# A two-block transformer kernel on one NeuronCore: the first feed-forward block moves from plain to Strassen products

## What is computed

```python
def swiglu(h, w_gate, w_up, w_down):
    return (jax.nn.silu(h @ w_gate) * (h @ w_up)) @ w_down

c_act = jax.nn.silu(c)
for l in range(DEPTH):                 # DEPTH = 2
    shift1, scale1, gate1, shift2, scale2, gate2 = jnp.split(c_act @ ada_w[l] + ada_b[l], 6, axis=-1)
    ...
    h = modulate(rms_norm(x, norm2_g[l]), shift2, scale2)
    x = x + gate2[:, None, :] * swiglu(h, ffn_w_gate[l], ffn_w_up[l], ffn_w_down[l])
```

## Time and profile before

| | |
|---|---|
| median of 3 runs | 1122.95 us (1122.59 to 1123.61) |
| the profiled execution | 1123.41 us |
| its span, first to last instruction | 1121.6 us |
| TensorE busy | 1059.0 us (94%) |
| VectorE busy | 577.9 us (52%) |
| ScalarE busy | 295.6 us (26%) |
| GpSimd busy | 64.0 us (6%) |
| mean granted TensorE clock | 0.987 |
| moved by DMA | 195.78 MB |

### The profile page before, as it was taken

The page is one execution under the profiler, slowest core; times in us unless marked ns, Lnnn a source line. Parts: engine busy times, 40 slices in busy tenths (PEclk is TensorE's granted clock), DMA queues, the critical chain, the costliest instruction groups (busy, mean ns, idle before and its releaser), DMA issues.

```text
span 1121.6 us, 21217 instructions
## 1 busy us (share of the span) xinstructions
PE 1059.0 (94%) x9229; PEld 910.9 (81%) x9229; DVE 577.9 (52%) x1112; ACT 295.6 (26%) x709; POOL 64.0 (6%) x84
## 2 busy tenths in 40 slices
PE   6878999999999999889999999999997899999997
PEld 4647888888888867678999999988886688887786
DVE  8986455344421727727766575335823551602632
ACT  6512410000000645623010000133322341202641
POOL 3010010110100100000000000000003000000000
PEclk9899999999999999999999999999998999999999
DMA  9995879999945334073544552443440003644220
GB/s 290 363 310 176 300 257 370 346 329 358 329 184 189 108 116 152 31 226 122 178 152 154 181 186 84 142 151 113 131 151 4 4 4 117 203 157 124 76 76 37
DMA packets 128742, 195.78 MB, mean 175 GB/s; under 512 B 4176, under 2 KB 114394, under 8 KB 122250
## 3 DMA queue, kind: packets, MB, share of 16 engines
q1 hardware_dynamic: 118218, 131.15, 36.7%
q0 software_dynamic: 10144, 62.92, 14.8%
q10 hardware_dynamic: 288, 0.36, 0.1%
HBM read 191.53 MB, written 1.05 MB: 172 GB/s over the span
## 4 chain that ended last, share of the span: by engine, by line
PE 82%; DVE 12%; ACT 3%; issue 2%; DMA 0%; SPq 0%; DVEq 0%; ACTq 0%
PE psum L743 48%; PE psum L1129 11%; PE psum L1215 7%; PE psum L1183 6%; DVE arena L1942 4%; PE psum L1018 2%; PE psum L1721 1%; ACT arena L2978 1%; DVE sq L1942 1%; DVE arena L1948 1%; DVE arena L2112 1%; PE psum L1696 1%; DVE arena L2206 1%; ACT sq L2978 1%; DVE arena L1945 1%
## 5 line engine op out<-in xcount | busy, mean ns | idle before, releaser
L2978 ACT ACTIVATE arena<-psum 128x512 f32<-128x512 f32 (+6 forms) x229 | 102.6, 475 | 574.6 <-PE psum L743 379.3
L743 PE MATMUL psum<-hT,ring 128*128 128x256 f32 x1072 | 239.4, 380 | 2.2 <-DVE hT L1948 1.3
L743 PEld LDWEIGHTS psum<-hT,ring 128*128 128x128 f32 x1072 | 201.3, 190 | 32.8 <-issue 6.5
L743 PE MATMUL psum<-arena 64*64 64x64 f32 (+6 forms) x2252 | 91.8, 252 | 16.4 <-issue 11.6
L1942 DVE TENSOR_TENSOR arena<-arena 128x512 f32<-128x512 f32 (+8 forms) x141 | 94.9, 696 | 11.3 <-PE psum L1183 8.6
L743 PE MATMUL psum<-hT,arena 128*128 128x256 f32 (+2 forms) x664 | 95.4, 323 | 4.9 <-DVE hT L1942 4.8
L743 PEld LDWEIGHTS psum<-hT,arena 128*128 128x128 f32 (+2 forms) x664 | 83.4, 180 | 16.5 <-issue 6.7
L743 PEld LDWEIGHTS psum<-arena 64*64 64x64 f32 (+3 forms) x2252 | 72.2, 150 | 30.3 <-issue 26.4
L743 PE MATMUL psum<-ring,arena 128*128 128x256 f32 (+2 forms) x288 | 73.3, 415 | 0.5 <-ACT arena L2978 0.5
L743 PEld LDWEIGHTS psum<-ring,arena 128*128 128x128 f32 x288 | 54.5, 190 | 18.1 <-issue 7.7
L1942 DVE TENSOR_TENSOR arena<-arena,psum 128x512 f32<-128x512 f32 (+2 forms) x56 | 30.7, 569 | 73.4 <-ACT arena L2978 41.1
(11 more groups left out here) (312 smaller groups left out, 1469.3 us busy)
## 6 DMA issues: line engine op xcount, KB each, us to landing
aring<-in_ada_w POOLq DMA_DIRECT2D x36, 1024.0 KB, 8.4
ring<-in_a_w_in SPq DMA_DIRECT2D x14, 1024.0 KB, 5.4
arena<-in_ffn_w_gate SPq DMA_DIRECT2D x12, 1024.0 KB, 5.4
arena<-in_ffn_w_up SPq DMA_DIRECT2D x12, 1024.0 KB, 8.3
ring<-in_ffn_w_down SPq DMA_DIRECT2D x11, 1024.0 KB, 6.8
ring<-in_ffn_w_gate SPq DMA_DIRECT2D x10, 1024.0 KB, 8.8
ring<-in_ffn_w_up SPq DMA_DIRECT2D x10, 1024.0 KB, 9.2
ring<-in_ada_w POOLq DMA_DIRECT2D x8, 1024.0 KB, 14.5
```

The lines of the kernel that those rows point to most:

```text
L743: return eng.matmul(dst, w, x, start=first, stop=last)
L2978: return eng.activation(dst, x, f, **k)
```

## The change

In the first feed-forward block, pairs 2, 4, 6, 8 and 10 and the whole down product are computed by the scheme of the second block. Pairs 0, 1, 3, 5, 7 and 9 stay plain. The down product no longer runs between the pairs but after all of them, with 12 panels instead of 11. VectorE takes the 36 modulation panels in other places: one behind the first chunk and two before the second, three beside each later plain pair, two beside each Strassen pair (28 by the end of pair 10), and two in each of the four output pairs of the down product. The TensorE steps of the modulation rows and columns move as well, and so do the places of `ada_bias`: the bias of block 3 from behind chunk 7 to the end of plain pair 5, that of block 4 to the end of pair 7, and that of block 5 to the end of pair 10. The sums of `hid` get other space, and in the second block the pools "a" and "b" change places.

```diff
-        HALVED = (1,)
+        HALVED = (0, 1)
+        FAST = {0: (2, 4, 6, 8, 10), 1: tuple(range(1, NDN))}
...
# TensorE
+            def whole_chunks(l, j, g, u):
+                for m in range(2):
+                    c = 2 * j + m
+                    eng.wait_ge(*next_bank(("gu", l, c)))
...
+                    last.then_inc(*fills(("gu", l, c)))
...
+                    if j not in FAST[l]:
+                        whole_chunks(l, j, g, u)
+                        beside(j)
+                        continue
+                    n, nth, pool = unit_of(l, j), nth_of(l, j), "ab"[FAST[l].index(j) % 2]
...
+            ROWS_AT, COLUMNS_AT = {3: 3, 5: 4, 9: 5}, {4: 3, 6: 4, 10: 5}
+            def ada_beside(j):
+                if j in ROWS_AT:
+                    ada_rows(ROWS_AT[j])
+                if j in COLUMNS_AT:
+                    row_columns(COLUMNS_AT[j], row_late, "a")
-            swiglu(0, 0, ada_beside)
+            def ada_beside_down(i, q):
+                if (i, q) == (0, 2):
+                    ada_rows(6)
+                if (i, q) == (1, 1):
+                    row_columns(6, row_late, "a")
+            swiglu_of_halves(0, 0, ada_beside, ada_beside_down)
...
# VectorE
+                    if j not in fast:
+                        for m in range(2):
+                            c = 2 * j + m
+                            combine_to(j + 1, m + 1)
+                            eng.wait_ge(*filled_at(("gu", l, c)))
+                            eng.wait_ge(done("silu_ready"), silus(l, c))
+                            tt(hid[:, c, :], hid[:, c, :], bank_of(("gu", l, c))[:, T:2 * T], ALU.mult)\
+                                .then_inc(*v.empties(("gu", l, c)))
+                            hid_done[0] = v.last
+                            beside(j, 1)
+                        combine_to(j + 1, 3)
+                        beside(j, 1)
...
+                        beside(j, 0)
...
+                    combine_to(j, 4)
...
+                    beside(j, 1)
+                    if j % 2 == 0 and j < NDN - 1:
                         combine_hidden(l, [j - 2, j - 1])
...
-            def ada_beside(c):
-                for _ in range(2 if c < 14 else 1):
+            def ada_beside(j, n):
+                for _ in range(n):
                     ada_panel()
-                if c in (7, 11, 15, 19):
-                    ada_bias({7: 3, 11: 4, 15: 5, 19: 6}[c])
-            swiglu(0, ada_beside)
+                if n == 0 and j in (5, 7, 10):
+                    ada_bias({5: 3, 7: 4, 10: 5}[j])
+            def ada_beside_down(i):
+                ada_panel()
+                ada_panel()
+                if i == 2:
+                    ada_bias(6)
+            swiglu_of_halves(0, 0, lambda i: None, ada_beside, ada_beside_down)
```

213 lines of the change are left out of this document (95 added, 118 removed).

## The result

The changed kernel takes **1133.22 us** (median of 6 runs, 1129.54 to 1137.12) against 1123.04 us of the kernel before (6 runs, 1122.59 to 1125.56). The ratio is 1.0087, with a 95% interval of 1.0060 to 1.0113. The prediction was 1123.8 us, with a range up to 1129.5: too low, and the result is outside.

The account below looks back on a forecast made before the run. TensorE was taken to bound both feed-forward blocks. Savings of -13.7, waits of +5.4, +5.8, +0.3 and +2.4, and +0.7 at the end gave +0.9 us: 1123.8 us on the median's footing, range 1119.0 to 1129.5.

Parts of the forecast that it names:

- What TensorE saves: First feed-forward block: five Strassen pairs save 6.5 us and the down product 7.2, together 13.7 us.
- The waits, pair by pair: TensorE waiting for VectorE in pairs 2, 4, 6, 8 and 10: 5.4, 0, 5.8, 0.3 and 2.4 us.
- the upper bounds: Waits with panel landings at 10.4 us, such as 6.8 in pair 2 and 4.5 in pair 10: whole kernel 1132 us.
- part 4: Pair 2: VectorE's fourth weight sum at 174.1 and PSUM sums at 175.3 us, wanted at 170.9: a loss of 4.4 us.
- What a wait costs: Waits in the first block's pairs were added to the sum at their length, with no term for a lower clock.
- The end, "hidden": After the down product: +0.7 us for longer outputs; POOL's 5.8 us load of `mem`, issued some nine us ahead, stays hidden.
- Behind the block nothing: After the first feed-forward block: no time lost; the second block's pool swap costs 0.
- saturation: Modulation loads in the block: landings of 10.4 us throughout set the pace, 1129 to 1132 us; chance 0.24.
- Early panels: Modulation panels land in 5.7 us throughout: 3.8 us saved, 1119.2 us; chance 0.22, shared with another rival.
- the estimate for the down product: Down product: VectorE needs 15.3 of TensorE's 17.2 us per output pair, starting one pair ahead: wait 0.

Follow-up runs that it names:

- run 13: Run 12's kernel with pair 1's third panel behind pair 2's reads of its half products, and the down product's first sums behind pair 10's reads: 1112.90 us, 0.9910.
- run 12: Run 7's kernel with the fourth part of the weight sums of pairs 2 and 10 ahead of the third panel of pairs 1 and 9: 1117.12 us, 0.9942.
- run 1: Changed kernel with the bias of modulation block 3 behind the product of chunk 10 instead of at the end of pair 5: 1125.82 us, 1.0012.
- run 3: Changed kernel with 31 unread 256-column filler matmuls at the waits of pairs 2, 6, 10 and ahead of the transposes of `mem`: 1133.03 us, 1.0083.
- run 2: Changed kernel with the down product's modulation panels three, three, two and none per output pair instead of two each: 1128.91 us, 1.0038.
- the second batch: Later measurements in which the changed kernel was run again, unaltered: 1130.47 us, 1.0069 against the kernel before.
- run 7: Changed kernel with the edits of run 1 and run 2 together: 1121.02 us, 0.9976.
- run 4: Changed kernel with POOL loading only a sixteenth of each modulation panel of the block, VectorE's instructions kept, output not the reference's: 1124.22 us, 0.9998.
- run 8: Run 7's kernel with all sums of a Strassen pair ahead of its modulation panels and the bias of block 4 early too: 1123.60 us, 1.0002.
- run 6: Run 3's kernel with fillers again, unaltered, in the same rounds as the changed kernel's repeat: 1131.20 us, 1.0059.
- run 10: Changed kernel with 62 one-column filler calls, 31 in pair 2 and 31 ahead of pair 6 (124 records more): 1140.85 us, 1.0146.
- run 14: Run 12's kernel again, unaltered, beside run 13: 1117.36 us, 0.9936.
- run 11: Changed kernel with only the 31 one-column filler calls ahead of pair 6 (62 records more): 1136.95 us, 1.0117.

## Why the prediction was wrong

By its own steps:

- **What TensorE saves: right.** Pairs without waits last 12.5 us and the down product from 303.2 to 373.8 is 68.8 plus its row and column. With nearly all waits gone (run 13) the block is 9.9 us shorter than before, of 13.7 that are there.
- **The waits, pair by pair: right.** Forecast 5.4, 0, 5.8, 0.3 and 2.4; measured 4.1, 0.4, 5.9, 1.1 and 3.2 (what each pair has over 12.5 us, less the low clock; its row or column step left out). The sum is 14.8 against 13.9. Places and releasers were as said. One reading was off: landings before the change reached 11.9 us (the load issued at 205.3 us), not 10.4, which the upper bounds left out; from pair 2 on the longest is now 9.3. For pair 2 it named part 4 and the reads together; run 12 and run 13 tell them apart: it was the reads.
- **What a wait costs: wrong, the main miss.** The sum counted a wait at its length. After the idle stretches of 3.0 to 5.8 us the granted clock was at the 1.2 GHz level for the next products: 5.8 us in the three pairs. Runs 1, 3 and 13 take it away, by taking away the wait or filling it. Each of them cost 1.4 to 1.6 times its length.
- **The end, "hidden": wrong, the second miss.** The prediction took `mem`'s issue from its place in the program, nine us ahead, and did not work out when the slots of panels 35 and 36 come free. They came free at 356.7 and 359.1 us, landed late, and the cover was gone: 2.4 us of wait, and then 4.0 us more for the products behind it, at the 1.2 GHz level. The tail is 6.4 us longer, where 0.7 was forecast. Run 2 removes the wait and 5.1 us of the tail.
- **Behind the block nothing: right.** The rest took 0.9 us less.

So +0.9 for the waits, +5.8 for the clock and +5.7 for the tail, 12.4 in all, make up the 12.3 us between the sum's +0.9 and the +13.2 at the kva projection. That is the account of one profiled execution. The median is 10.2 us above before, and 7.4 in the second batch (1130.47 against 1123.07), where the profiled one is again slower, with a span 13.8 us longer. Executions differ in how much low clock they meet: of the twelve there, the three fastest (1126.1 to 1128.0 us) had a mean clock of 0.984 to 0.987, the three slowest (1136.3 to 1137.9) 0.976 to 0.981. So the two misses are sized here for executions a little slower than the median. That they are the causes rests on runs 1, 2 and 7, whose medians fell with them.

Of the rivals, saturation gave 1129 to 1132 us and so lay next to the result, for the wrong reason. It needed landings of about 9.5 us on; between 157 and 304 us their median was 7.8 (24 loads, the longest 9.3), against 7.9 before (28 loads), and DMA fell from 0.98 to between 0.77 and 0.91 in the windows with pairs. What run 4 took away were waits behind landings of ordinary length, which the sum had counted. Early panels did not come either. Run 8 shows the weak side of the estimate for the down product: VectorE has little slack there (15.3 of 17.2 us by the prediction's own count), and its lead can be lost.

Not settled: why the fillers of runs 3 and 6 shorten the traced block and not the median, why run 10's median is 5.6 us above its profiled execution, and what decides, for waits of the same length, whether the clock falls.

## What to carry to other kernels

Where TensorE bounds a stretch at full clock, price a new wait of a few us at its length plus what the clock takes afterwards, some 2 us where it falls. When an engine that was idle gets work that TensorE waits for, write down for each wait what stands in its queue ahead of it, and move everything that can land late, or that nobody wants soon, behind the reads and sums that are wanted: that order was worth 20 us here (run 13 against the changed kernel), and turned a loss of 10 into a gain of 10. And for a load that counts as hidden, follow its slot back to who frees it, not its place in the program.

## What the runs showed of the hardware

- Nearly all waits of 3 to 6 us in a block of 128-column products were followed by products at the 1.2 GHz level, and most shorter ones (1.4, 2.0, 2.3, 2.5 us in runs 2, 12 and 14) were not. The length alone does not tell: in the second trace of the changed kernel 2.1 us in pair 10 were followed by a product of 2.94 us, and the 3.55 us in run 8 by products at full clock. Where the clock is kept, a wait that gets a little shorter can bring much more: in run 12 pair 2 waits 0.7 us less than in run 7, and the block is 2.5 us shorter.
- TensorE's instruction supply is a cost of its own where products are short: the 64x64 products of a section of 80 us wait 11.6 to 15.6 us for it in the thirteen traces without that shift, and 16.4 to 17.0 with 62 records more ahead of them. At the same clock the shift cost 3.5 to 4.5 us, about half of what the fillers under test had saved in the block. Fillers are not free, even within a wait.
- Small products are not small: a float32 call of one column, two records, took 0.26 to 0.33 us (8.2 to 10.2 for 31). Nor do they keep the clock up: from 222.5 to 226.0 us of run 11 it was 1.00, and 0.50 from there to 232.5, while they ran without a pause.
